# SSD scan on one core: where the exponentials of the decay matrix are taken, and by which engine

## What is computed

```python
cum = jnp.cumsum(dtc * a, axis=1)
xdt = xc * dtc[..., None]
diff = cum[:, :, None, :] - cum[:, None, :, :]
lmat = jnp.where(tri, jnp.exp(jnp.where(tri, diff, 0.0)), 0.0)
y = jnp.einsum('btsh,bshp->bthp', cb * lmat, xdt) \
    + jnp.einsum('bthn,bhpn->bthp', ch, h) * jnp.exp(cum)[..., None]
decay_out = jnp.exp(cum[:, -1:, :] - cum)
h = h * jnp.exp(cum[:, -1])[:, :, None, None] \
    + jnp.einsum('bshn,bshp->bhpn', bh * decay_out[..., None], xdt)
```

## Time and profile before

| | us |
|---|---|
| median of 3 runs | 2124.19 |
| lowest and highest | 2122.76 and 2125.1 |
| the profiled execution | 2121.8 |
| its span, first to last instruction | 2120.0 |

### The profile page before, as it was taken

How to read it: one execution, slowest core, us unless ns; L and a number is a source line. 1 busy time by engine, 2 the same in 40 slices (tenths; PEclk the granted TensorE clock), 3 DMA queues, 4 the chain that set the end, 5 groups by cost and what they waited for, 6 DMA issues and landing times. The chain is left out here.

```text
span 2120.0 us, 26779 instructions
## 1 busy us (share of the span) xinstructions
PE 1833.1 (86%) x11378; PEld 1350.9 (64%) x11378; DVE 738.8 (35%) x1206; ACT 545.1 (26%) x1038; POOL 340.4 (16%) x229
## 2 busy tenths in 40 slices
PE   4399949779988899999886879997999999977795
PEld 4244537556666599999774557774678845534794
DVE  1311110246555377503763231124201134432524
ACT  1400111145445532222442100025311112320004
POOL 1011000001010123223774311100000000010410
PEclk9699979889999999999997879998999999988898
DMA  9101083100000011110001463432111010014312
GB/s 341 79 0 69 1 192 100 41 23 1 1 1 1 5 31 50 50 41 14 1 1 33 139 206 110 163 127 89 40 40 40 1 40 1 1 32 139 122 41 82
DMA packets 130715, 132.05 MB, mean 62 GB/s; under 512 B 16166, under 2 KB 108872, under 8 KB 129956
## 3 DMA queue, kind: packets, MB, share of 16 engines
q1 hardware_dynamic: 109380, 105.07, 16.0%
q10 hardware_dynamic: 20864, 25.17, 3.5%
q0 software_dynamic: 352, 0.10, 0.1%
HBM read 104.96 MB, written 27.43 MB: 62 GB/s over the span
## 5 line engine op out<-in xcount | busy, mean ns | idle before, releaser
L155 PE MATMUL banks<-w_attn,h_T 128*128 128x512 f32 (+5 forms) x432 | 161.5, 536 | 0.0
L155 PE MATMUL banks<-h_T_rest,w_ssd_high 128*128 128x352 f32 x480 | 155.1, 323 | 0.0
L155 PE MATMUL banks<-h_T_high,w_ssd_rest 128*128 128x352 f32 x480 | 154.6, 322 | 0.0
L155 PE MATMUL banks<-h_T_high,w_ssd_high 128*128 128x352 f32 x480 | 154.3, 321 | 0.1
L155 PEld LDWEIGHTS banks<-w_attn,h_T 128*128 128x128 f32 (+1 forms) x432 | 78.8, 184 | 81.4 <-issue 64.5
L155 PE MATMUL banks<-w_r,h_T 128*128 128x512 f32 (+1 forms) x288 | 128.6, 600 | 0.0
L155 PE MATMUL banks<-w_qkv,h_T 128*128 128x256 f32 (+1 forms) x576 | 125.6, 380 | 0.5 <-ACT h_T L2146 0.5
L155 PEld LDWEIGHTS banks<-w_qkv,h_T 128*128 128x128 f32 (+1 forms) x576 | 103.7, 181 | 22.6 <-issue 2.6
L1149 DVE TENSOR_REDUCE neg_max_att<-banks 128x1 f32<-128x640 f32 (+7 forms) x128 | 89.2, 702 | 73.1 <-PE banks L155 72.7
L155 PE MATMUL banks<-h_T,w_qkv 128*128 128x352 f32 x384 | 114.5, 459 | 0.0
L155 PE MATMUL banks<-conv_T,out_even_w 128*128 128x352 f32 x288 | 92.6, 472 | 14.4 <-DMA out_even_w<-in_w_out_even_dram 13.1
(11 more groups left out here) (436 smaller groups left out, 3279.1 us busy)
## 6 DMA issues: line engine op xcount, KB each, us to landing
out_even_w_mod<-in_w_mod_dram ACTq DMA_DIRECT2D x8, 2048.0 KB, 9.6
w_ssd<-in_w_in_even_dram SPq DMA_DIRECT2D x20, 512.0 KB, 3.9
h_T<-x_T_save SPq DMA_DIRECT2D x2, 4224.0 KB, 14.1
w_qkv<-in_w_in_odd_dram SPq DMA_DIRECT2D x8, 1024.0 KB, 5.4
x_T_save<-x_T SPq DMA_DIRECT2D x1, 4224.0 KB, 24.2
x_T_save<-h_T SPq DMA_DIRECT2D x1, 4224.0 KB, 19.2
xin<-in_x_prompt_dram SPq DMA_DIRECT2D x2, 2048.0 KB, 15.1
h_T<-in_w_mod_dram SPq DMA_DIRECT2D x2, 2048.0 KB, 25.3
```

The lines of the kernel that those rows point to most:

```text
L155: return nc.tensor.matmul(out, lhsT, rhs, start=start, stop=stop, skip_group_check=True)
```

## The change

The subtraction on DVE goes. ACT reads the banks of `cum0` and `cum1` itself and takes exp(cum_t + bias), where the bias is minus cum_s. As a bias is one value per partition and instruction, and cum_s differs by head, ACT makes one instruction of 128 columns for each head: 8 for each half, 16 in a pass, where it had 2 of 1024 columns. DVE gets one small operation more, the negation of the 16 columns of sums into a new tile `neg_cum`, in front of the one that raises `small`. The banks of `cum0` and `cum1` are now taken by ACT, and `weights` waits for that; `L_ready` goes. ACT also waits, from the third pass on, until `intra` of two passes before has read the buffer of L. TensorE's program stays the same but for the semaphore that tells that the banks are free; POOL's stays the same.

```diff
--- before.py
+++ after.py
@@ -1422,7 +1422,7 @@
 
     UNITS = ("z", "inter", "intra", "upd", "yT")
     AHEAD = ("cb", "xs", "cum0", "cum1")
-    TAKERS = {"cb": ("dve", "act"), "xs": ("act",), "cum0": ("dve",), "cum1": ("dve",), "z": ("act",), "inter": ("dve",),
+    TAKERS = {"cb": ("dve", "act"), "xs": ("act",), "cum0": ("act",), "cum1": ("act",), "z": ("act",), "inter": ("dve",),
               "yT": ("dve",), "intra": ("dve",), "upd": ("dve",)}
     with ExitStack() as ctx:
         def sb(name, shape, dt=F32):
@@ -1433,12 +1433,12 @@
         xdt, xdt2, y, zs = (sb(s, [P, 2, SI]) for s in ("x_dt", "x_dt_decayed", "y_rows", "silu_z_b"))
         L, xsb = e.scan_decay, e.scan_xs
         h, hdec = S.h, sb("h_decayed", [P, SI])
-        ss = sb("y_norm", [P, 2, 1])
+        ss, neg = sb("y_norm", [P, 2, 1]), sb("neg_cum", [P, 2, SH])
         out = e.stored["ssd_state"]
         done = {u: new_sem(nc, f"scan_{u}_done") for u in AHEAD + UNITS}
         taken = {(u, t): new_sem(nc, f"scan_{u}_taken_{t}") for u in AHEAD + UNITS for t in TAKERS[u]}
-        names = ("small_ready", "decays_ready", "L_ready", "W_ready", "xdt_ready", "xdt2_ready", "hdec_ready", "y_gated", "y_squared", "var_ready", "std_ready", "yn_ready", "h_ready", "h_out")
-        small, decays, L_ready, W_ready, xdt_ready, xdt2_ready, hdec_ready, y_gated, y_squared, var_ready, std_ready, yn_ready, h_ready, h_out = \
+        names = ("small_ready", "decays_ready", "W_ready", "xdt_ready", "xdt2_ready", "hdec_ready", "y_gated", "y_squared", "var_ready", "std_ready", "yn_ready", "h_ready", "h_out")
+        small, decays, W_ready, xdt_ready, xdt2_ready, hdec_ready, y_gated, y_squared, var_ready, std_ready, yn_ready, h_ready, h_out = \
             (new_sem(nc, "scan_" + s) for s in names)
         order = [(u, 0) for u in AHEAD]
         for i in range(NTP):
@@ -1530,8 +1530,13 @@
                     act.wait_ge(small, i + 1)
                     nc.scalar.activation(sm[:, i % 2, :, :], sm[:, i % 2, :, :], ACT.Exp).then_inc(decays, 1)
                     for c in range(2):
-                        act.wait_ge(taken[f"cum{c}", "dve"], i + 1)
-                        nc.scalar.activation(L[:, i % 2, c, :, :], L[:, i % 2, c, :, :], ACT.Exp).then_inc(L_ready, 1)
+                        act.wait_ge(done[f"cum{c}"], i + 1)
+                        if i >= 2:
+                            act.wait_ge(done["intra"], i - 1)
+                        for hh in range(8):
+                            last = nc.scalar.activation(L[:, i % 2, c, hh, :], e.ps[:, pair[(f"cum{c}", i)] + hh // 4, hh % 4 * P:(hh % 4 + 1) * P], ACT.Exp,
+                                                        bias=neg[:, i % 2, 8 * c + hh:8 * c + hh + 1])
+                        last.then_inc(taken[f"cum{c}", "act"], 1)
 
                 def gate_rows(i):
                     act.wait_ge(done["z"], i + 1)
@@ -1616,15 +1621,12 @@
                     dve.wait_ge(taken["cb", "dve"], i + 1)
                     nc.vector.tensor_copy(sm[:, k, 0, :], cc[:, k, 256:272])
                     nc.vector.tensor_copy(sm[:, k, 2, :], cc[:, k, 272:288])
+                    nc.vector.tensor_scalar(neg[:, k, :], cc[:, k, 256:272], -1.0, None, ALU.mult)
                     nc.vector.tensor_tensor(sm[:, k, 1, :], cc[:, k, 272:288], cc[:, k, 256:272], ALU.subtract).then_inc(small, 1)
-                    for c in range(2):
-                        dve.wait_ge(done[f"cum{c}"], i + 1)
-                        nc.vector.tensor_tensor(L[:, k, c, :, :], both(f"cum{c}", i).rearrange("p b (h t) -> p (b h) t", h=4),
-                                                cc[:, k, 256 + 8 * c:264 + 8 * c][:, :, None].broadcast_to([P, 8, P]), ALU.subtract).then_inc(taken[f"cum{c}", "dve"], 1)
 
                 def weights(i, c):
                     k = i % 2
-                    dve.wait_ge(L_ready, 2 * i + c + 1)
+                    dve.wait_ge(taken[f"cum{c}", "act"], i + 1)
                     nc.vector.tensor_tensor(L[:, k, c, :, :], L[:, k, c, :, :], cc[:, k, c * P:(c + 1) * P][:, None, :].broadcast_to([P, 8, P]), ALU.mult).then_inc(W_ready, 1)
 
                 differences(0)
```

## The result

| | before | after |
|---|---|---|
| median | 2123.53 us (12 runs, 2121.3 to 2132.03) | 2130.8 us (12 runs, 2124.33 to 2139.63) |
| profiled execution, its span | 2121.8, 2120.0 us | 2131.7, 2129.9 us |
| block of the scan, barrier to barrier | 164.76 us | 170.60 us |

The ratio of the runs is 1.0029, with a 95% interval of 1.0015 to 1.0043. I had forecast 2126.1 us and no change that can be measured. It is slower, by 0.3%, and it lies outside my range of 2122.8 to 2129.5 us.

A forecast was written before the change was run, and what follows sets the result against it. TensorE's own work plus a 3.33 us idle chain through DVE and ACT was taken to bound each scan pass. Running passes 0, start +1.4 and +0.5, gave 2124.19 + 1.9 = 2126.1 us; range 2122.8 to 2129.5 us.

The forecast's parts named there:

- Running passes: 0: Running scan passes: subtractions leaving DVE gain nothing and ACT's heads stay covered, so TensorE waits for no head; 0 us.
- the spacing taken from rows 9: ACT's per-head exponentials of 128 columns follow one another at 0.26 us, from trace rows; eight take 2.2 us, sixteen 4.3.
- The negation: DVE's added 16-column operation: 0.1 us unhindered; held up by POOL it could end 1.9 us later, still 0 in running passes.
- the cover of 1.3 us: Running pass with negation delayed by POOL: half free at 52.2, TensorE comes at 1053.50, so no wait.
- my lower bound: First pass: small operations end 1.7 us sooner as DVE reaches them earlier; first term -0.3, second 0.
- The start, +1.4 and +0.5: First two scan passes lack cover: ACT's heads free the banks late, delaying TensorE 1.4 us, then another 0.5 us.
- the 0.73 us: Scan start in the kernel before: TensorE waits 0.73 us for a subtraction before first intra; ACT inherits the wait.
- The clock behind the start: First scan pass: the forecast sum had no term for a clock fall behind the new stall.
- the 3.33 us stretch: TensorE's idle time before the transposes in a running pass, waiting on a DVE and ACT chain; the clock falls behind it.
- The rival I had priced at 1.6 us a pass: Clock redraws in running passes: none at full clock, +3.5 in all, chance 0.12; four more, -4.7, chance 0.04.
- The sum: Whole kernel: 0 for running passes plus 1.4 and 0.5 at the start, +1.9 us; upper bound +3.7.
- The rival on the other side, heads of over 0.43 us: ACT becomes the bound: TensorE waits every pass; at 0.6 us a head +12, 2136 us; chance 0.06.

The follow-up runs named there:

- the second trace: The changed kernel run once more with no edit: block 170.32 us, first state update at 25.77 us, median +4.4 us, ratio 1.0024 against the kernel before.
- the filled one: Changed kernel with the first inter's four products issued twice: block 167.31 us, first update 22.93 us, median +6.6 us, ratio 1.0030 against the kernel before.
- the changed kernel with the early norm factor: Changed kernel with DVE computing the previous pass's norm factor ahead of adding the intra product: block 140.83 us, median 2102.25 us, ratio 0.9899.
- its order mended: Changed kernel with early norm factor, negation straight from the bank and first eight heads before the small decays' exponential: block 137.18 us, median 2097.48 us, ratio 0.9873.
- another kernel: Kernel before with only pass 1's matrix taken by ACT head by head: idle 1.18 us, block 170.43 us, median +8.2 us, ratio 1.0038.

## Why the prediction was wrong, point by point

**Running passes: 0.** Right as to waits. TensorE's products waited for no head in them, and the 27.3 us in front of the transposes stayed. Sixteen heads took 4.21 us against the 4.3 I had worked out, (4.21 - 0.37) / 15 = 0.256 us from one to the next, so the spacing taken from rows 9 held. The estimate of 294 ns from the Trainium skill, ScalarE: Activation LUTs, What ACT_TABLE_LOAD costs, was 0.04 us too high for this shape.

**The negation.** Right in kind: DVE's negation was held up by POOL in the first two passes and in three of the running ones, and in these the cover of 1.3 us hid it. At the start there is no cover. DVE came to the first pass's small operations 1.9 us sooner than before, as my lower bound had it, and the negation lost it again: it took 1.88 us, to 998.55, where POOL's L1574 ends at 998.52, so the small operations ended as late as before, as the sum had assumed. Two rows of the changed kernel's DVE timeline, from the first pass and a running one:

```profile
996.67 1.88 DVE L1624 TENSOR_SCALAR neg_cum<-cb_cum 128x16 f32<-128x16 f32 x1
...
1114.31 1.89 DVE L1624 TENSOR_SCALAR neg_cum<-cb_cum 128x16 f32<-128x16 f32 x1
```

**The start, +1.4 and +0.5.** The sizes were good: `intra` of the first pass came 17.33 - 16.20 = 1.13 us later, and between the first two state updates lie 14.77 us where it was 14.24, +0.53. Together 1.7 of my 1.9. One reading under it was wrong: the 0.73 us that I gave as a wait of TensorE in the kernel before is that of its weight load, and the product behind it had no idle time.

**The clock behind the start: the step that failed.** I priced the stall by its own length. In the changed kernel the first update came 4.34 us later, and the stall is 1.13 of it; the other 3.21 are `intra` and `upd` at the lower clock (in the second trace 2.84). Two kernels show the price by themselves: the filled one, with the same `intra` start and no idle time, gave 3.21 us back, and the changed kernel with the early norm factor, with the same stall and no fall, 3.20. My sum had put this term at nothing. That it came is in part chance, as far as three traces can tell: with the stall alone, as in that third trace, the start would have cost what I had forecast. I had read of a clock that falls behind the 3.33 us stretch, had used it for those stretches alone, and never asked what an idle time of another length, which the change would newly make, does to the clock. I had also counted the stall as 1.4 us against TensorE's arrival of before, while TensorE itself came 0.7 us sooner, so it idled 1.77.

**The clock in the running passes.** The rival I had priced at 1.6 us a pass. Behind the first update the changed block is 170.60 - 26.14 = 144.46 us long against 142.96, +1.50, of which 0.53 is the second stall. The remaining 0.97 goes by the clock, as the products' waits are the same: one pass of 21.48 us, more than any before, with the clock at 0.50 for six us (from 1027 to 1033), and again one of 18.63. The second trace had none short, and came to about the same.

**The sum.** 1.13 + 3.21 + 0.53 + 0.97 = 5.84 us, for this pair of traces. My forecast of 1.9 holds the first and third term, with 0.2 too much. The range ended 5.3 us above the median of before, since it had only the longest heads and one lost pass in it; a fall in pass 0 was no case of mine. The rival on the other side, heads of over 0.43 us, didn't come; the other side was reached by another way. I had also priced it too low: by the way in which I got 2.3 and 1.4 us at the start for 0.37 us a head, 0.6 us gives 4.1 and 3.2, and not 4.5 together.

## What to carry to other kernels

A new stall of TensorE isn't priced by its length alone, since a fall of the clock may follow it: look whether anything works in its place, and ask what the granted clock does behind it, first of all where the pipeline fills and there is no cover. When an engine takes over the freeing of a bank, its first act must not stand behind a signal that comes by way of a third engine; here moving the negation and the small exponential gave back the whole loss. And the engine shares pointed at nothing: what bounded each pass was two tiny DVE operations queued behind a state update, worth 26 us by the block (164.76 to 138.54). That the change itself (DVE 15 us less busy) is worth anything once those are out of the way is not shown: 1.4 us by the block, with its order mended, and nothing by the median.

## What the runs showed of the hardware that I had not expected

An idle time of 1.77 us between long stretches of dense products at 2.4 GHz was followed, 2 to 3 us after work resumed, by 6 to 7 us at 1.2 GHz, in both traces of the changed kernel, and one of 1.18 us in another kernel as well. But 1.78 us in a third trace of the same first pass was not, nor were 1.03 and 0.50 us. Such a fall cost 2.8 to 3.2 us. The falls behind the 3.33 us of a running pass mostly cost 1.64; one of them, with the clock at 0.50 for six us, cost 21.48 - 18.63 = 2.85. The two traces of the kernel before agreed to 0.02 us in the block under study and differed by 8.2 us elsewhere, of which 2.7 us are one norm block at a mean clock of 0.76 instead of 0.83.
